# Eight RMS norms: squares summed into one column per token half, a broadcast row through TensorE, and two weight tiles begun together

## What is computed

```python
def _rmsnorm(x, gain):
    xf = x.astype(jnp.float32)
    y = xf * lax.rsqrt(jnp.mean(xf * xf, axis=-1, keepdims=True) + NORM_EPS)
    return (y * gain.astype(jnp.float32)).astype(x.dtype)
...
h = rms_norm(x, g) * (1.0 + scale) + shift      # the norms of the second block
x = x + gate * mixer(h, ...)
```

## Time and profile before

| | us |
|---|---|
| median of three timed runs | 2727.39 |
| the profiled execution, device time | 2713.75 |
| its span | 2711.9 |
| TensorE busy (PE, share of the span) | 2518.0 (93%) |
| VectorE busy | 1723.9 (64%) |
| ScalarE busy | 1206.9 (45%) |
| GpSimd busy | 1242.2 (46%) |
| mean granted TensorE clock | 0.96 |

### The profile page before, as it was taken

The page is one execution under the profiler, slowest core; times in us unless marked ns, Lnnn a source line. Parts: engine busy times, 40 slices in busy tenths (PEclk is TensorE's granted clock), DMA queues, the critical chain, the costliest instruction groups (busy, mean ns, idle before and its releaser), DMA issues.

```text
span 2711.9 us, 45525 instructions
## 1 busy us (share of the span) xinstructions
PE 2518.0 (93%) x17530; PEld 2326.1 (86%) x17530; DVE 1723.9 (64%) x3023; ACT 1206.9 (45%) x2063; POOL 1242.2 (46%) x506
## 2 busy tenths in 40 slices
PE   7998899859689999999999999788999999999998
PEld 6997899849689999998888889657999999988887
DVE  5558485568827966666777762862695666555555
ACT  5334433324445544444444444244454444454453
POOL 4347688516267986662000015405799666300000
PEclk8899999889789999999999998889999999999999
DMA  4224487744145554446777773303555444566664
GB/s 168 86 87 149 158 247 241 263 152 151 49 154 179 186 167 147 147 149 197 259 257 256 256 234 124 102 23 114 175 181 177 148 148 148 163 191 191 193 191 143
DMA packets 125334, 457.82 MB, mean 169 GB/s; under 512 B 13904, under 2 KB 14288, under 8 KB 124752
## 3 DMA queue, kind: packets, MB, share of 16 engines
q1 hardware_dynamic: 124848, 450.73, 51.9%
q10 hardware_dynamic: 288, 4.33, 0.4%
HBM read 453.95 MB, written 1.05 MB: 168 GB/s over the span
## 4 chain that ended last, share of the span: by engine, by line
PE 72%; DVE 8%; POOL 8%; issue 6%; DMA 3%; ACT 2%; SPq 0%; POOLq 0%; DVEq 0%; ACTq 0%
PE ms L1153 26%; PE mm L1115 17%; PE mm L714 16%; POOL low L1588 8%; PE ms L1135 4%; PE mm L721 3%; DVE work L1621 1%; DVE work L1624 1%; PE mm L732 1%; PE mm L744 1%; DMA ring<-w_ffn_up 1%; DVE work L1918 1%; DMA ring<-w_ffn_down 1%; ACT high L1283 1%; DVE work L1627 1%
## 5 line engine op out<-in xcount | busy, mean ns | idle before, releaser
L1588 POOL TENSOR_TENSOR low<-ring,high 128x1024 fp32r<-128x1024 f32 (+1 forms) x502 | 1242.0, 2486 | 1102.4 <-ACT high L1283 922.1
L1485 ACT ACTIVATE high<-ring 128x1024 fp32r<-128x1024 f32 x506 | 535.7, 1059 | 357.2 <-PE ms L1153 319.3
L1115 PE MATMUL mm<-hs,high 128*128 128x256 f32 x4096 | 524.0, 281 | 3.4 <-ACT high L1283 3.4
L1153 PE MATMUL ms<-high,wts 128*128 128x512 f32 x2048 | 510.5, 391 | 0.4 <-DVE wts L2075 0.4
L1115 PEld LDWEIGHTS mm<-hs,high 128*128 128x128 f32 x4096 | 490.1, 188 | 3.8 <-issue 3.8
L2084 DVE TENSOR_TENSOR low<-ring,high 128x1024 fp32r<-128x1024 f32 x256 | 313.3, 1225 | 249.3 <-ACT high L1485 249.1
L1153 PEld LDWEIGHTS ms<-high,wts 128*128 128x128 f32 x2048 | 384.1, 188 | 84.6 <-DVE wts L2075 0.8
L1283 ACT ACTIVATE high<-ring 128x1024 fp32r<-128x1024 f32 (+1 forms) x252 | 259.1, 1032 | 261.3 <-PE mm L714 117.2
L714 PE MATMUL mm<-hs,high 128*128 128x256 f32 x2608 | 344.1, 286 | 28.8 <-ACT high L1283 16.8
L714 PEld LDWEIGHTS mm<-hs,high 128*128 128x128 f32 x2608 | 325.2, 195 | 33.2 <-ACT high L1283 18.6
L1115 PE MATMUL mm<-hs,low 128*128 128x256 f32 x2048 | 278.5, 278 | 11.0 <-POOL low L1588 10.8
(11 more groups left out here) (276 smaller groups left out, 2869.8 us busy)
## 6 DMA issues: line engine op xcount, KB each, us to landing
ring<-w_peer_experts SPq DMA_DIRECT2D x512, 512.0 KB, 3.9
ring<-w_mod SPq DMA_DIRECT2D x48, 512.0 KB, 4.2
ring<-w_late_mods SPq DMA_DIRECT2D x48, 512.0 KB, 4.5
ring<-w_ffn_up SPq DMA_DIRECT2D x44, 512.0 KB, 4.5
ring<-w_peer_q SPq DMA_DIRECT2D x32, 512.0 KB, 3.5
ring<-w_lru_in SPq DMA_DIRECT2D x22, 512.0 KB, 4.1
ring<-w_gates SPq DMA_DIRECT2D x16, 512.0 KB, 3.5
ring<-w_ffn_down SPq DMA_DIRECT2D x16, 512.0 KB, 3.9
```

Of the source, the lines that this page charges most:

```text
L1115: ins_ = pe.matmul(mm[:, s_ % BANKS, 0:T], w_[:, k * P:(k + 1) * P], hs[:, b_, k, :], start=pass_ == 0 and k == 0, stop=pass_ == 2 and k = ...
L1153: ins_ = pe.matmul(ms[:, 2 * c + half, :], wts[:, s_ % 3, b_, c * P:(c + 1) * P], v_[:, half * 512:(half + 1) * 512], start=s_ == 0 and pa ...
L1485: act.activation(high[:, (q0 + i) % CUT, :], ring[:, n_ % RAW, :], ACT.Copy) \
L1588: pool.tensor_tensor(low[0:rows, cut_slot, 0:width], ring[0:rows, raw_slot, 0:width], high[0:rows, cut_slot, 0:width].bitcast(F32), ALU.su ...
```

## The change

The squares become the weights of the sum and one column of ones the moving operand: for each of the 8 groups and each of the two token halves c one fp32 matmul into `dst_[:, c:c + 1]`, so that the 128 tokens of a half lie on the partitions of one column. ScalarE waits for this sum itself and takes the root of 128x2 with scale 1/D and the new bias column `eps`; VectorE takes the reciprocal of 128x2; TensorE turns each of the two columns into a row of 128 with `across`, in the second half of the same bank; VectorE scales x from this row in PSUM. The bank is released behind the eight scalings by a memset, and another memset signals `x_done` for norm 3. TensorE's program now stands at the wait for the reciprocal before anything that follows the sum.

`first_products` takes two tiles at once: both tiles' matmuls at each high part, then both with low weights, then both at each low part; each tile is signalled at its last matmul. For lru_in it is called with one tile. As the second tile is needed with the first, `ahead` before norms 2 and 5 cuts tiles 0 and 1.

```diff
--- before.py
+++ after.py
@@ -122,7 +122,7 @@
 VECS = [("g_mix", 8), ("g_ffn", 8), ("g_ple", 8), ("g_final", 8), ("gdn_norm", 1), ("ml_norm", 4),
         ("conv", 48), ("norms2", 32), ("mod_b", 96), ("c", 8), ("gate_bias", 16), ("a_log", 4),
         ("lru_conv", 4 * RT), ("lru_conv_b", RT), ("ra_b", RT), ("ri_b", RT), ("lam", RT),
-        ("fox_fb", 16), ("fox_qg", 1), ("fox_kg", 1)]
+        ("fox_fb", 16), ("fox_qg", 1), ("fox_kg", 1), ("eps", 1)]
 VEC0 = {}
 _n = 0
 for _name, _w in VECS:
@@ -413,7 +413,8 @@
         vec = sb("vec", [P, VECW])
         wsmall = sb("wsmall", [P, KD, 16])
         wfox = sb("wfox", [P, KD, 16])
-        rstd = sb("rstd", [P, T])
+        rms = sb("rms", [P, TT])
+        rstd = sb("rstd", [P, TT])
         mod = sb("mod", [P, 24 * MODS])
         modg = sb("modg", [P, KD * MODS])
         csilu = sb("csilu", [P, KD])
@@ -726,24 +727,35 @@
                 n = OUT0[f"norm{i}"]
                 if i == 0:
                     pe.wait_ge(sem("con_loaded"), 16)
-                dst_ = bank(n)[:, 0:T]
+                dst_ = bank(n)
                 for k in range(KD):
                     pe.wait_ge(sem("norm_squares"), KD * i + k + 1)
-                    ins = pe.matmul(dst_, ones, hf[:, k, :], start=k == 0, stop=k == KD - 1)
+                    for c in range(TT):
+                        ins = pe.matmul(dst_[:, c:c + 1], hf[:, k, c * P:(c + 1) * P], ones[:, 0:1],
+                                        start=k == 0 and c == 0, stop=k == KD - 1, skip_group_check=True)
                 S.did(ins, "outs")
-                return i
-
-            def first_product(dst_, q, ws, i):
+                pe.wait_ge(sem("norm_inverse"), i + 1)
+                for c in range(TT):
+                    ins = across(dst_[:, T + c * P:T + (c + 1) * P], rstd[:, c:c + 1])
+                S.did(ins, "norm_rows")
+
+            def first_products(dsts, tiles_, i):
 
                 for s_, (a_, b_) in enumerate(((0, 0), (1, 0), (0, 1))):
                     if s_ == 1:
-                        low_ready(q)
+                        for dst_, (q, ws) in zip(dsts, tiles_):
+                            low_ready(q)
+                            for k in range(KD):
+                                pe.matmul(dst_, ws[k][1], hs[:, 0, k, :], start=False, stop=False,
+                                          skip_group_check=True)
+                        continue
                     for k in range(KD):
-                        if s_ != 1:
-                            pe.wait_ge(sem("h_low" if b_ else "h_high"), KD * H_NORMS.index(i) + k + 1)
-                        ins_ = pe.matmul(dst_, ws[k][a_], hs[:, b_, k, :], start=s_ == 0 and k == 0,
-                                         stop=s_ == 2 and k == KD - 1, skip_group_check=True)
-                return ins_
+                        pe.wait_ge(sem("h_low" if b_ else "h_high"), KD * H_NORMS.index(i) + k + 1)
+                        for dst_, (q, ws) in zip(dsts, tiles_):
+                            ins_ = pe.matmul(dst_, ws[k][0], hs[:, b_, k, :], start=s_ == 0 and k == 0,
+                                             stop=s_ == 2 and k == KD - 1, skip_group_check=True)
+                            if s_ == 2 and k == KD - 1:
+                                S.did(ins_, "outs")
 
             def groups_of(act_):
 
@@ -755,12 +767,15 @@
 
                 acts = hgroups if acts is None else acts
                 rows = len(acts)
+                begun = []
                 for t in range(first, tiles):
                     q, wh, wl = parts_of(stage, t)
                     ws = [(wh[:, k * m:(k + 1) * m], wl[:, k * m:(k + 1) * m]) for k in range(rows)]
                     dst_ = bank(OUT0[stage] + t if out_of is None else out_of(t))[0:m, 0:T]
-                    if t == 0 and after_norm is not None:
-                        S.did(first_product(dst_, q, ws, after_norm), "outs")
+                    if t < 2 and after_norm is not None:
+                        begun.append((dst_, (q, ws)))
+                        if t == 1:
+                            first_products(*zip(*begun), after_norm)
                     else:
                         S.did(three_passes(dst_, q, ws, acts), "outs")
 
@@ -1058,7 +1073,7 @@
                     ws = [(wh[:, k * P:(k + 1) * P], wl[:, k * P:(k + 1) * P]) for k in range(KD)]
                     dst = bank(lru_out_of(kind, j))[:, 0:T]
                     if j == 0 and b == 0:
-                        S.did(first_product(dst, q, ws, 4), "outs")
+                        first_products([dst], [(q, ws)], 4)
                     else:
                         S.did(three_passes(dst, q, ws, hgroups), "outs")
                 if j >= 2:
@@ -1251,8 +1266,12 @@
                     S.did(act.activation(hf[:, k, :], x[:, k, :], ACT.Square), "norm_squares")
 
             def root(i):
-                act.wait_ge(sem("norm_inverse"), i + 1)
-                S.did(act.activation(rstd[:, :], rstd[:, :], ACT.Sqrt), "norm_rstd")
+                if i == 0:
+                    act.wait_ge(sem("vec_loaded"), 16)
+                n = OUT0[f"norm{i}"]
+                out_ready(act, n)
+                S.did(act.activation(rms[:, :], mm[:, BANK_OF[n], 0:TT], ACT.Sqrt, bias=v("eps"), scale=1.0 / D),
+                      "norm_root")
 
             def high_parts(i):
 
@@ -1295,7 +1314,6 @@
             ahead("qkv", 0)
             root(0)
             high_parts(0)
-            act.wait_ge(sem("vec_loaded"), 16)
             S.did(act.activation(expa, v("a_log"), ACT.Exp), "expa_ready")
             S.did(act.activation(csilu[:, :], v("c"), ACT.Silu), "csilu_ready")
 
@@ -1404,7 +1422,7 @@
                 evacuate(OUT0["ffn_up"] + 2 * j, up[:, j % 2, :], ACT.Silu)
             ahead("ffn_down", 23)
             squares(2, "ffn_down")
-            ahead("ple_gate", 0, 0)
+            ahead("ple_gate", 0, 1)
             root(2)
             high_parts(2)
             act.dma_start(lgw, lru_gate_w).then_inc(sem("lru_gates_loaded"), 16)
@@ -1464,7 +1482,7 @@
                     ahead("lru_out", 2 * KD - 1)
                 squares(5 + 2 * L, "fox_out" if L else "lru_out")
                 if not L:
-                    ahead("peer0_q", 0, 0)
+                    ahead("peer0_q", 0, 1)
                 root(5 + 2 * L)
                 high_parts(5 + 2 * L)
                 for j in range(16):
@@ -1633,19 +1651,22 @@
             def norm(i, gain):
 
                 n = OUT0[f"norm{i}"]
-                src = bank(n)
+                dve.wait_ge(sem("norm_root"), i + 1)
                 if i >= 1:
                     S.settle()
-                ts(rstd[:, :], src, 1.0 / D, EPS, ALU.mult, ALU.add, taken(n))
-                S.settle()
-                S.did(dve.reciprocal(rstd[:, :], rstd[:, :]), "norm_inverse")
-                dve.wait_ge(sem("norm_rstd"), i + 1)
+                S.did(dve.reciprocal(rstd[:, :], rms[:, :]), "norm_inverse")
+                dve.wait_ge(sem("norm_rows"), i + 1)
+                rows = mm[:, BANK_OF[n], T:2 * T]
                 if i == 0:
                     dve.wait_ge(sem("vec_loaded"), 16)
                 for k in range(KD):
 
-                    dst, name = (x, "x_done" if k == KD - 1 else None) if i == 3 else (hf, "h_scaled")
-                    stt(dst[:, k, :], x[:, k, :], gain[:, k:k + 1], rstd[:, :], ALU.mult, ALU.mult, name)
+                    dst, name = (x, None) if i == 3 else (hf, "h_scaled")
+                    stt(dst[:, k, :], x[:, k, :], gain[:, k:k + 1], rows, ALU.mult, ALU.mult, name)
+                S.settle()
+                if i == 3:
+                    S.did(dve.memset(tiny[:, 510:511], 0.0), "x_done")
+                S.did(dve.memset(tiny[:, 509:510], 0.0), taken(n))
                 if i == 3:
                     return
 
@@ -2390,6 +2411,7 @@
     put("fox_fb", a["l1_fox_f_b_2"][None, :])
     put("fox_qg", np.concatenate([a["l1_fox_q_norm_g_2"]] * 2)[:, None])
     put("fox_kg", np.concatenate([a["l1_fox_k_norm_g_2"]] * 2)[:, None])
+    put("eps", EPS)
 
     wide = np.zeros((2, RT * P, RT * P), np.float32)
     for n in range(NBLK):
```

## The result

The changed kernel takes 2749.4 us (median of 8 runs, 2738.5 to 2753.7), and the kernel before 2720.4 (eight runs, the three from the beginning among them). The ratio, taken from the means, is 1.0095, with a 95% interval of 1.007 to 1.012: it is slower by about 26 us (29 between the medians), where 14.5 less were forecast. The profiled execution took 2753.0 (span 2751.1).

What follows compares the result with a forecast made beforehand. TensorE carries 72% of the last-ending chain; time is won where it waits or runs at half clock. Norm terms -2.5-0.5+2.0-0.7-8.2-2.3-2.3 = -14.5 take 2727.4 to 2712.9, say 2713 us; range 2703 to 2724.

Steps and rivals of the forecast that it cites:

- Slower: Rival: TensorE stays at 1.2 GHz behind the one-column sums; 2742 us, chance 0.06.
- Norm 5: Tile 1 cut earlier, so low parts no longer collide with GpSimd (under 6 us) and tile 1 isn't cold: -8.2 us.
- Small prices: Steps from sum to first scaling: root 0.21, reciprocal 0.18, row 0.65 to 1.05; 1.3 warm, 1.65 cold, against 2.7 us.
- The sum's clock: One-column sums cost +0.1 us warm, +2.4 all cold; half the gain, 0.65, taken for norms 1 and 7.
- rival "clock": Sparse sums delay the clock's return, so pairs gain nothing in norms 0, 6 and 7; 2718 us, chance 0.12.
- The pair: Both tiles' first passes run while ScalarE makes high parts: 7.55 us for both, against 9.15 (norm 7) and 9.95 (norm 6).
- norms 6 and 7: Norm 6: cold sum cancels the chain's gain, pair gives -2.3 us; norm 7: first product at 1871.6, -2.3 us.
- Norm 0: First scaling later, but eight scalings take 3.25 us, not 5.56; first product about 18.4: -2.5 us.
- Norms 3 and 4: Norm 3 +0.6 us from a half-cold sum; norm 4's first scaling at 597.4 instead of 598.10; together -0.7 us.
- rival "port held": Scaling whose second tensor is in PSUM stops for GpSimd too; -11.8, 2715.6 us, chance 0.09.
- Table loads: Norms 0, 2 and 4: priced at 1.28 us each; by the skill's 2.7, each 1.4 later, 4.2 in all.
- Norm 2: ple_gate tile 1 cut before the root; sum of mod0 queues behind the row, ends near 526.5, not 520.1: +2.0 us (0 to 3.5).

Runs made afterwards that it cites:

- e1: The changed kernel with 960 unused bytes behind the small rstd, so all behind it lies where it did before the change; 2711.7 us, ratio 0.9959 to before.
- e2: The kernel before with rstd moved behind wts, so mod to wts lie at the changed kernel's byte offsets; 2757.8 us, ratio 1.0136 to before.
- e7: The kernel before with the pair of tiles alone, second tile cut ahead at norms 2 and 5; 2713.3 us, ratio 0.9961 to before.
- e6: e1 without the pair of tiles: new sums, root, reciprocal, row and PSUM scaling stay; 2716.6 us, ratio 0.9982 to before.
- e11: e1 with 64 unused bytes between hs and wts, putting wts a multiple of 256 bytes from high; 2707.4 us, ratio 0.9920 to before.
- e12: e11 with norm 2 unpaired, one ple_gate tile cut ahead and worked alone; 2701.1 us, ratio 0.9917 to before.
- e4: The kernel before with 64 unused bytes ahead of ring, moving every tensor up and keeping their distances; 2722.2 us in one run.
- e5: e2 with 25 blocks of 64 matmuls behind its end, each with other byte shifts of weights and moving operand; its total says nothing.

## Why the prediction was wrong

**The step that failed** is the frame of the sum: it ran over the norms, and everything outside them was taken at the cost of before. The change also moved hs and parts, and 256-column products pay for that on every one of the tiles, 0.120 in place of 0.113 to 0.118. That term, +35 to +38 us (e1, e2), is missing; with it -14.5 would have been about +22, and +26 was measured. The diff showed the cause (a tensor in the middle of the allocation shrinks), and the 0.113 a product of the earlier trace rows stand above 0.107, half of the 0.213 that I read at half the clock. I took the 0.113 for a constant, and asked neither where hs would lie nor what the 0.006 were. Why the distance matters to TensorE no run here shows.

**The rivals** didn't hold it either. "Slower" named TensorE at half clock behind the sums; the mean granted clock is 0.954 after against 0.96, and the loss sits in products at full clock. The range ended at 2724.

**What was forecast for the norms** is borne out once the places are held: e1 is 11.1 us below before (7 to 15) against 14.5. By step:

- Norm 5, -8.2: -7.3, and by the named cause. In e1 two tiles are cut at once and the low parts take 5.39, not the 7.46 of the earlier trace rows; tile 1 no longer waits cold. It is the pair's doing: e7 alone gives -7.0. "Under 6 us" held.

```profile
770.10 1.99 ACT L1303 ACTIVATE high<-ring 128x1024 fp32r<-128x1024 f32 x2
...
778.77 5.39 DVE L1646 SCALAR_TENSOR_TENSOR hs<-scratch,mod,hs 128x256 fp32r<-128x256 f32 x8
...
782.73 1.99 PE L756 MATMUL mm<-hs,high 128*128 128x256 f32 x16
```

- Small prices: root 0.21 forecast, 0.26 measured; reciprocal 0.18, 0.17; the row 0.65 to 1.05, 1.23 in every norm, above both bounds. From the root's start to the first scaling it is 1.78, where 1.3 to 1.65 were forecast from the sum's end. Norm 1 of e1:

```profile
304.78 0.26 ACT L1274 ACTIVATE rms<-mm,vec 128x2 f32<-128x2 f32 x1 [2.36 <-PE mm L735]
305.08 0.17 DVE L1658 RECIPROCAL rstd<-rms 128x2 f32<-128x2 f32 x1 [7.03 <-ACT rms L1274]
305.30 1.23 PE L829 MATMUL mm<-con,rstd 128*128 128x128 f32 x4 [0.55 <-DVE rstd L1658]
306.56 3.22 DVE L1646 SCALAR_TENSOR_TENSOR scratch<-x,vec,mm 128x256 f32<-128x256 f32 x8 [1.32 <-PE mm L829]
```

- The sum's clock. I took half of it cold at norms 1 and 7. The windows of e1 (length, busy us by engine, granted clock, DMA) show the lower level, 1.2 GHz, for most of norm 1's sum (299.12 to 304.75) and of norm 7's (1865.57 to 1870.93):

```profile
300.60:303.60 3.00, 3.00 (x16) 3.00 (x16) 0.00 (x0) 1.81 (x3) 0.45 (x1) 0.50 0.40 160
...
1867.00:1872.60 5.60, 5.05 (x25) 4.77 (x24) 0.17 (x1) 2.11 (x4) 0.55 (x1) 0.53 0.41 140
```

  In e1 the sum of norm 1 ends 3.6 behind the last square, 1.7 before the change. Cold sums and the dear row take back what the short root and reciprocal give. Of the 1.8 that the chain alone loses at norm 1, only 0.5 lie ahead of the first product; in the other 1.4 the two tiles behind it take 10.0 in place of 8.65, as the clock came back 7.9 us behind the first product in e6 and 5.0 before. That is what the rival "clock" described, at this one norm; with the pair (e1) it came back after 3.3. Norm 7 missed by 1.3 for the late sum.
- The pair, 7.55 forecast from the first product on: well sized. In e1 it took 7.04 at norm 1, 8.07 at norm 5, 7.66 at norm 6 and 7.26 at norm 7 (1873.91 to 1881.17, the start of the next tile; to the end of the last product, as the 9.15 of before was read, each is 0.16 more). What failed at norms 6 and 7 is the start of the first product, 0.3 and 0.7 later behind the squares than before, where 0 and 0.65 earlier were forecast. Norm 0 missed by 1.6: the same in e1 took 7.7, but from 19.71 on, where 18.4 was forecast; in e11 the first product started at 18.86 and the norm gained 2.2.
- Norms 3 and 4, -0.7: +0.3. Norm 3 lost 1.2 (0.6 forecast), from its last square to norm 4's, and norm 4 gave back 0.9.
- PSUM scaling, rival "port held": refuted. It took 3.22 in every norm, also in norm 0 of the changed kernel, where GpSimd was cutting until 19.17, 1.4 us into it; with its row in SBUF it had taken 5.56:

```profile
14.52 4.65 POOL L1606 TENSOR_TENSOR low<-ring,high 128x1024 fp32r<-128x1024 f32 x2
14.71 1.28 ACT L1273 ACT_TABLE_LOAD   x1
16.00 0.26 ACT L1273 ACTIVATE rms<-mm,vec 128x2 f32<-128x2 f32 x1
...
17.77 3.22 DVE L1645 SCALAR_TENSOR_TENSOR scratch<-x,vec,mm 128x256 f32<-128x256 f32 x8 [1.31 <-PE mm L828]
```

- Table loads: 1.28 each, 14.71 above among them, and the root follows 0.01 behind. The Trainium skill (ScalarE: Activation LUTs, "What ACT_TABLE_LOAD costs") has about 1283 ns for the load itself, as here, and 1380 ns of drain besides, 2.66 us in all; the prediction set only that total against the 1.28. In norm 0 no drain shows on either side of the load, so the extra 1.4 did not come.
- Norm 2, +2.0: +1.6, with the mods behind the row as described. But the price is the second tile's, not theirs: e6 and e12 keep the mods behind the row and cut one tile ahead, and their stretch is 0.9 and 1.5 below before; e7 has the pair alone and lies 1.8 above.

## What to carry to other kernels

A smaller tensor is not a local edit: it moves all that is allocated behind it, so write down the addresses of both kernels before costing a diff, and hold them with padding when a change is to be judged. Compare groups that the change doesn't touch first; if their mean has moved, the cause isn't in the diff's arithmetic. And an engine's idle gap is only worth filling if what the filler holds up isn't on the path to the next load.

## What the runs showed of the hardware

- 256-column fp32r matmuls with new weights each time start every 113.4, 118 or 120 ns at full clock according to the distance of the two operands' bytes in a partition: 0 modulo 256 gives 120, 64 and 128 give 118 and 119, 192 gives 113.4 or 118, and either can last over several blocks. 512-column ones do best at 0 and 240 (227) and worst at 192 and 208 (233 and 235). The absolute place doesn't count (e4, and both shifted by 128 in e5). The Trainium skill (TensorE: Matmul & The Clock Gate, "Back-to-back issue gap") gives 262 cycles for a matmul of 256 columns by itself, 109 ns at 2.4 GHz, and says that in a stream the weight load counts too; it has no term for the operands' places. No block here ran below 113.
- Sums over one moving column can have TensorE busy throughout (3.00 of 3.00 us in norm 1 above) and yet run at the lower clock, where the 256-column sum of before kept 1.00 in norm 1 (299.0 to 302.5). They don't always: in norm 2 of the changed kernel such a sum was busy for 3.50 of 3.50 us at 1.00 (521.2 to 524.7).
- A VectorE scaling with its row in PSUM didn't stop for a cutting GpSimd (3.22, above); with both tensors in SBUF it did (5.56).
